# Latent norms, rotary keys and S5's angles and step table worked out under the first projection

## What is computed

```python
h = rmsnorm(x, norm_mix[layer])
z = h @ e_w_in[li]                      # 1024 -> 512 (u) + 384 (xq) + 256 (xkv) + 32 (kr)
u, xq, xkv, kr = z[..., :o1], z[..., o1:o2], z[..., o2:o3], z[..., o3:]
y_s5, hr, hi = s5_mixer(u, ...)         # diagonal state space: h[t] = a * h[t-1] + x[t], a complex
...
def mla_project(xq, xkv, kr, pos, q_norm, w_uq, kv_norm):
    q = jnp.einsum('ntr,rhd->nthd', rmsnorm(xq, q_norm), w_uq)
    ...
    ckv = rmsnorm(xkv, kv_norm)
    k_rope = rope(kr, pos, MLA_THETA)
...
def s5_mixer(...):
    dt = jnp.exp(log_dt)[:, None]
    mag = jnp.exp(lr * dt)
    ar = mag * jnp.cos(li * dt)
    ai = mag * jnp.sin(li * dt)
```

## Time and profile before

| | us |
|---|---|
| median of 3 runs | 3492.07 (3490.07 to 3496.64) |
| profiled execution | 3496.9 |
| its span, from the first to the last instruction | 3494.7 |
| PE busy | 3119.3 (89%) |
| DVE busy | 1784.7 (51%) |
| ACT busy | 693.3 (20%) |
| POOL busy | 878.2 (25%) |

### The profile page before, as it was taken

The page is one execution under the profiler, slowest core; times in us unless marked ns, Lnnn a source line. Parts: engine busy times, 40 slices in busy tenths (PEclk is TensorE's granted clock), DMA queues, the critical chain, the costliest instruction groups (busy, mean ns, idle before and its releaser), DMA issues. The chain is left out here.

```text
span 3494.7 us, 58782 instructions
## 1 busy us (share of the span) xinstructions
PE 3119.3 (89%) x21927; PEld 2794.6 (80%) x21927; DVE 1784.7 (51%) x2928; ACT 693.3 (20%) x1443; POOL 878.2 (25%) x496
## 2 busy tenths in 40 slices
PE   7736788888888888899999999999879999999996
PEld 7623465666676666899999999999549999999996
DVE  4288264554645555365244343566774643525254
ACT  2010132333323332121000000110551210000001
POOL 3100000000001110444343434442004444344332
PEclk9867899999989998999999999999989999999998
DMA  2000100010056664211111111120211111111112
GB/s 99 12 14 15 42 12 13 0 37 0 0 161 195 195 194 122 97 57 47 44 48 44 49 40 55 39 67 25 80 55 51 55 39 51 44 53 41 49 41 70
DMA packets 129070, 205.44 MB, mean 59 GB/s; under 512 B 14817, under 2 KB 95713, under 8 KB 128258
## 3 DMA queue, kind: packets, MB, share of 16 engines
q1 hardware_dynamic: 127810, 199.81, 18.9%
q10 hardware_dynamic: 1152, 4.23, 0.3%
HBM read 189.61 MB, written 6.25 MB: 56 GB/s over the span
## 5 line engine op out<-in xcount | busy, mean ns | idle before, releaser
L136 PE MATMUL ps_trunk_out<-sb_h_hi,sb_slab_hi 128*128 128x344 f32 x2400 | 768.0, 320 | 0.0
L137 PE MATMUL ps_trunk_out<-sb_h_hi,sb_slab_lo 128*128 128x344 f32 x2400 | 764.8, 319 | 0.0
L138 PE MATMUL ps_trunk_out<-sb_h_lo,sb_slab_hi 128*128 128x344 f32 x2400 | 764.4, 319 | 0.0
L120 POOL TENSOR_TENSOR sb_slab_hi<-sb_slab_raw,sb_ones 128x1024 fp32r<-128x1024 f32 (+3 forms) x214 | 345.7, 1616 | 1361.2 <-PE ps_trunk_out L138 1051.6
L122 POOL TENSOR_TENSOR sb_slab_lo<-sb_slab_raw,sb_slab_hi 128x1024 fp32r<-128x1024 f32 (+3 forms) x214 | 485.7, 2270 | 16.8
L137 PEld LDWEIGHTS ps_trunk_out<-sb_h_hi,sb_slab_lo 128*128 128x128 f32 x2400 | 450.4, 188 | 0.6
L136 PEld LDWEIGHTS ps_trunk_out<-sb_h_hi,sb_slab_hi 128*128 128x128 f32 x2400 | 450.3, 188 | 0.6
L138 PEld LDWEIGHTS ps_trunk_out<-sb_h_lo,sb_slab_hi 128*128 128x128 f32 x2400 | 450.4, 188 | 0.0
L1314 POOL TENSOR_TENSOR sb_dec_kr<-sb_dec_ck,sb_ones 128x256 f32<-128x256 f32 x64 | 46.7, 729 | 1199.4 <-DMA sb_dec_ck<-cache 1103.1
L136 PE MATMUL ps_trunk_out<-sb_ffn_a_hi,sb_slab_hi 128*128 128x344 f32 x1056 | 336.9, 319 | 4.9 <-DVEq L1586 4.9
L138 PE MATMUL ps_trunk_out<-sb_ffn_a_lo,sb_slab_hi 128*128 128x344 f32 x1056 | 337.9, 320 | 0.0
(11 more groups left out here) (386 smaller groups left out, 5163.2 us busy)
## 6 DMA issues: line engine op xcount, KB each, us to landing
sb_dec_ck<-cache SPq DMA_DIRECT2D x512, 144.0 KB, 2.4
sb_slab_raw<-f_w_gu SPq DMA_DIRECT2D x88, 512.0 KB, 3.5
sb_slab_raw<-f_w_down SPq DMA_DIRECT2D x32, 384.0 KB, 3.1
sb_slab_raw<-f_w_down SPq DMA_DIRECT2D x32, 320.0 KB, 2.9
sb_slab_raw<-e_w_out SPq DMA_DIRECT2D x24, 256.0 KB, 2.6
sb_slab_raw<-o_w_in SPq DMA_DIRECT2D x12, 512.0 KB, 3.4
sb_slab_raw<-e_w_in SPq DMA_DIRECT2D x10, 512.0 KB, 3.3
sb_x_first<-x SPq DMA_DIRECT2D x8, 516.0 KB, 8.4
```

Source lines behind the costliest of these rows:

```text
L120: nc.gpsimd.tensor_tensor(hi, raw, one, ALU.mult).then_inc(self.hi_done[s], 1)
L136: nc.tensor.matmul(out[:, t, 0:TT], a, x_hi(k)[:, cols], start=k == 0, stop=False)
L137: nc.tensor.matmul(out[:, t, 0:TT], b, x_hi(k)[:, cols], start=False, stop=False)
L138: last = nc.tensor.matmul(out[:, t, 0:TT], a, x_lo(k)[:, cols], start=False, stop=k == kc - 1)
```

## The change

The three pieces of work leave their places and stand in the block of the first projection. The ten tiles come in the sequence 4 to 9, then 0 to 3 (`tile(q) = (q + 4) % 10`), so both latents and the key come first. The loops over tiles are written out.

- SP loads S5's parameters first of all, issues the key's part of the rotary table (32 partitions, `kr_rot`) when the step table is done, and stores latent and key in this block.
- ACT and DVE work out the angles before the first norm.
- DVE doubles the table between evacuations: six doublings behind the first, the seventh behind the second, and the eighth in two halves behind the third and fourth. The result goes where x lay. Then come the sums of squares of the latents (PE's sums over the partitions stand inside tiles 6 and 7), the scalings behind evacuations 5 and 6, and the key's rotation behind evacuation 7. The swap of the halves is now a shuffle on DVE and not a product on PE.
- S5's block keeps the rest. The key rotation's block is gone, and the attention's block loads the full rotary table between mask and weights.

```diff
+        pc, psn, nps = (small("s5_" + n, [P, NPOW, NTILE5]) for n in ("pc", "ps", "nps"))
...
+            swap_lanes = [q ^ 16 for q in range(32)]
+            thirds = [slice(t * TT, (t + 1) * TT) for t in range(3)]
+            evacuated = lambda eng, q: eng.wait_ge(slabs.free[q % 2], n0 + q // 2 + 2)
...
             with nc.Block() as block:
                 @block.sync
                 def _(sp):
+                    sp.dma_start(par[:, :, :], A["s5_par"]).then_inc(par_in, 16)
                     for k in range(KD):
                         sp.dma_start(x[:, k, :], A["x"][k]).then_inc(norm_x_in[k], 16)
                         if k < 2:
-                            slabs.load(sp, k, n0, KD, A["e_w_in"][k])
-                    with sp.Fori(0, 4) as i:
-                        for s in range(2):
-                            slabs.load(sp, s, i + (n0 + 1), KD,
-                                       A["e_w_in"][bass.ds(i * 2 + s + 2, 1)].rearrange("a p k m -> p (a k) m"))
+                            slabs.load(sp, k, n0, KD, A["e_w_in"][tile(k)])
+                    for q in range(2, 10):
+                        slabs.load(sp, q % 2, q // 2 + n0, KD, A["e_w_in"][tile(q)])
+                        if q == 7:
+                            sp.wait_ge(tab_done, 1)
+                            sp.dma_start(kr_rot[:, :, :], A["rot_mla"][0:ROPE]).then_inc(kr_in, 16)
+                    sp.wait_ge(lat_done, 2)
+                    store(sp, O["ckv"].rearrange("c p t -> p c t"), z[:, 7:9, :])
+                    sp.wait_ge(kr_done, 1)
+                    store(sp, O["krope"], z[0:ROPE, 9, :])
...
-                    with pe.Fori(0, 4) as i:
-                        for s in range(2):
-                            slabs.products(pe, s, i + (n0 + 1), KD, hi, lo)
+                    def lat_sums(i, a, *ts):
+                        pe.wait_ge(lat_added, (2, 3)[i])
+                        for t in ts:
+                            if t == 2:
+                                pe.wait_ge(lat_root, 3 * i + 1)
+                            nc.tensor.matmul(tot(t), ones[:, :], a[:, thirds[t]], start=True, stop=True).then_inc(lat_sum, 1)
+                    hooks = {0: paced(pe, 0),
+                             1: {1: lambda: (norm_sums(pe, 0, acc, tot, 0), norm_sums(pe, 0, acc, tot, 1)),
+                                 4: lambda: norm_sums(pe, 0, acc, tot, 2)},
+                             6: {1: lambda: lat_sums(0, q_acc, 0, 1), 4: lambda: lat_sums(0, q_acc, 2)},
+                             7: {3: lambda: lat_sums(1, kv_acc, 0, 1), 6: lambda: lat_sums(1, kv_acc, 2)}}
+                    for q in range(10):
+                        if q == 6:
+                            pe.wait_ge(norm_root, 3)
+                        if q == 7:
+                            pe.wait_ge(lat_root, 3)
+                        slabs.products(pe, q % 2, n0 + q // 2, KD, hi, lo, hooks[q] if q in hooks else ())
                 @block.scalar
...
+                    ch = Chain(act, act_chain, chain_at["act"])
+                    act.wait_ge(par_in, 16)
+                    nc.scalar.activation(dtv, par[:, 2, :], ACT.Exp).then_inc(dt_done, 1)
+                    act.wait_ge(th_done, 1)
...
+                    nc.scalar.activation(pc[:, :, :], pc[:, :, :], ACT.Sin, scale=-1.0,
+                                         bias=halfpi[:, 0:1]).then_inc(trig_done, 1)
+                    chain_at["act"] = ch.n
                     for k in range(KD):
                         act.wait_ge(norm_x_in[k], 16)
                         norm_act(act, 0, k, x[:, k, :], gain(k), acc[:, :], sq[:, :])
                     norm_roots(act, 0, tot, D)
+                    for q, dst in enumerate((q_acc, q_r, kv_r, kv_acc, sq)):
+                        evacuated(act, q)
+                        if q == 4:
+                            act.wait_ge(tab_done, 1)
+                        nc.scalar.activation(dst[:, :], z[:, 4 + q, :], ACT.Square).then_inc(lat_sq, 1)
+                    for i, (r, width) in enumerate(((q_r, QL), (kv_r, KVL))):
+                        for t in range(3):
+                            act.wait_ge(lat_sum, 3 * i + t + 1)
...
                     for k in range(KD):
                         norm_dve(dve, 0, k, x[:, k, :], gain(k), acc[:, :], sq[:, :])
                     norm_inverse(dve, ch, 0)
+                    def evacuate(q):
+                        dve.wait_ge(slabs.mm_done[q % 2], n0 + q // 2 + 2)
+                        V.tensor_tensor(v3(z[:, tile(q), :]), slabs.out[:, q % 2, :, 0:TT], v3(rstd),
+                                        ALU.mult).then_inc(slabs.free[q % 2], 1)
+                    def double(j, n0, n1):
+                        n = n1 - n0
+                        pcb, psb = (v[:, 2 + j, :].unsqueeze(2).broadcast_to((P, NTILE5, n)) for v in (pc, psn))
+                        w = [t[:, 0:NTILE5 * n].rearrange("p (a b) -> p a b", b=n) for t in tmp]
+                        c0, s0 = tab[:, 0, :, n0:n1], tab[:, 1, :, n0:n1]
+                        step = 1 << j
+                        V.tensor_tensor(w[0], c0, pcb, ALU.mult)
+                        V.tensor_tensor(w[1], s0, psb, ALU.mult)
+                        V.tensor_tensor(w[2], c0, psb, ALU.mult)
+                        tt(w[3], s0, pcb, ALU.mult)
+                        V.tensor_tensor(tab[:, 0, :, step + n0:step + n1], w[0], w[1], ALU.subtract)
+                        tt(tab[:, 1, :, step + n0:step + n1], w[2], w[3], ALU.add)
+                    def added(i, a, s, n):
+                        dve.wait_ge(lat_sq, n)
+                        if i:
+                            dve.wait_ge(lat_added, i)
+                        V.tensor_tensor(a[:, :], a[:, :], s[:, :], ALU.add).then_inc(lat_added, 1)
+                    def scale(i, r, c0, cols, g0):
+                        for t in range(3):
+                            dve.wait_ge(lat_root, 3 * i + t + 1)
+                            ch.mark(V.reciprocal(r[:, thirds[t]], r[:, thirds[t]]))
+                        ch.settle()
+                        for c in range(cols):
+                            m = V.scalar_tensor_tensor(out=z[:, c0 + c, :], in0=z[:, c0 + c, :], scalar=gq[:, g0 + c:g0 + c + 1],
+                                                       in1=r[:, :], op0=ALU.mult, op1=ALU.mult)
+                        m.then_inc(lat_done, 1)
+                    evacuate(0)
+                    dve.wait_ge(trig_done, 1)
+                    V.memset(tab[:, 0, :, 0:1], 1.0)
+                    ch.link(V.memset(tab[:, 1, :, 0:1], 0.0))
+                    for j in range(6):
+                        double(j, 0, 1 << j)
+                    evacuate(1)
+                    double(6, 0, 64)
+                    evacuate(2)
+                    double(7, 0, 64)
+                    evacuate(3)
+                    double(7, 64, 128)
+                    dve.sem_inc(tab_done, 1)
+                    added(0, q_acc, q_r, 2)
+                    added(1, q_acc, kv_r, 3)
+                    evacuate(4)
+                    added(2, kv_acc, sq, 5)
+                    evacuate(5)
+                    scale(0, q_r, 4, 3, 0)
+                    evacuate(6)
+                    scale(1, kv_r, 7, 2, 3)
+                    evacuate(7)
+                    dve.wait_ge(kr_in, 16)
+                    kr = z[0:ROPE, 9, :]
+                    ch.link(V.stream_shuffle(kr_s[:, :], kr, swap_lanes))
+                    tt(kr_t[:, :], kr, kr_rot[:, 0, :], ALU.mult)
+                    tt(kr_s[:, :], kr_s[:, :], kr_rot[:, 1, :], ALU.mult)
+                    V.tensor_tensor(kr, kr_t[:, :], kr_s[:, :], ALU.add).then_inc(kr_done, 1)
+                    evacuate(8)
+                    evacuate(9)
                     chain_at["dve"] = ch.n
...
-        norm_phase("n_q", lambda k: z[:, 4 + k, :], 3, QL, lambda k: gq[:, k:k + 1], plain=lambda k: z[:, 4 + k, :])
-        norm_phase("n_kv", lambda k: z[:, 7 + k, :], 2, KVL, lambda k: gq[:, 3 + k:4 + k], plain=lambda k: z[:, 7 + k, :])
...
                 @block.sync
                 def _(sp):
-                    for dst, src in ((par[:, :, :], "s5_par"), (bw[:, :, :, :], "s5_b"), (cw[:, :, :, :], "s5_c"),
+                    for dst, src in ((bw[:, :, :, :], "s5_b"), (cw[:, :, :, :], "s5_c"),
                                      (dskip[:, :], "s5_d"), (h0[:, :, :, :], "s5_h0")):
...
                     dve.wait_ge(ca_done, 1)
-                    for j in range(8):
-                        n = 1 << j
-                        pcb, psb = (v[:, 2 + j, :].unsqueeze(2).broadcast_to((P, NTILE5, n)) for v in (pc, psn))
-                        w = [t[:, 0:NTILE5 * n].rearrange("p (a b) -> p a b", b=n) for t in tm]
-                        tc0, ts0 = tab[:, 0, :, 0:n], tab[:, 1, :, 0:n]
-                        V.tensor_tensor(w[0], tc0, pcb, ALU.mult)
-                        V.tensor_tensor(w[1], ts0, psb, ALU.mult)
```

(15 more changed lines are left out.)

199 lines of the change are left out of this document (68 added, 131 removed).

## The result

| | kernel before | changed kernel |
|---|---|---|
| median, us | 3491.07 (3489.93 to 3496.64) | 3429.17 (3425.60 to 3433.76) |
| profiled execution, us (its span) | 3496.64 (3494.7) | 3433.76 (3431.9) |
| ratio after/before | | 0.9823, 95% interval 0.9811 to 0.9835 |

A forecast was written before the change was run, and what follows sets the result against it. TensorE (PE) bounds the kernel (89% busy) and the first projection; terms -37.5 - 0.4 - 25.0 - 9.7 + 1.3 + 4.1 + 7.7 + 1.6 + 0.4 = -57.5 us; 3492.07 - 57.5 = 3434.6 us, range 3422 to 3446.

The forecast's parts named there:

- (a): Behind the first projection: the two latent norms leave the path, -37.5 us.
- (b): S5's angles behind its loads: taking them out gains nothing, one DMA issue fewer ahead of the loads gives -0.4 us.
- (c): Ahead of S5's first step: the table's 48 DVE operations go, but DVE then waits for PE's first states, -25.0 us.
- (d): Between gate and attention: the key rotation's block goes, but the rotary table now queues ahead of the weights, -9.7 us.
- (e): Ahead of the first norm: exponentials, angles and sines now stand before ACT's first product, +1.3 us, bounds 0 and 3.0.
- the replay: Ahead of the first norm: DVE's and POOL's turns replayed with ACT 3.0 us late, third low part 1.3 us later.
- (f): Latent sums: three products with ones inside each of two projection tiles, +4.1 us for both.
- (g): First projection: doublings blocked by POOL's splits make evacuations late; PE waits +7.7, slow clock +1.6, later wait +0.4 us.
- R1: First projection: doublings not blocked, or POOL gives way, so the late evacuations cost nothing; 3425 us, chance 15%.
- R2: Terms at their bad ends, with load and weights sharing the queue slowly; gain 52, 3440 us, chance 12%.
- R3: First projection: PE's clock falls at tile 3's wait and doesn't return; slower than before, 3500 us, chance 2%.
- R4: End of projection: the second norm's end or the rotation hangs behind the last tile; gain about 40, 3452 us, chance 3%.

## Why the prediction was right, and where not

- **Norms (a), -37.5.** 43.43 - 5.66 = 37.8 with the load's front of (b) in it, and 37.1 with the norms put back. Right.
- **S5 behind the loads (b), -0.4.** Last evacuation to landing is 5.66 us in the changed kernel (5.5 to 6.0 over the nine other profiles without a norm there and without this load) and 6.3 with the angles' parameters loaded there again. The angles themselves cost nothing there (73.6 us with and without). Right.
- **Table (c), -25.0.** 73.68 - 48.49 = 25.2, and 25.1 by putting it back. The step that made it 25 and not 30.9, that PE's first states were beneath the table and would be late next, is the 5.56-us wait at 207.58. One slip in a bound: by its own rates, 64 x 0.066 = 4.2 us from 226.25, the states would have ended 1.4 us earlier, not 1.5.
- **Key rotation (d), -9.7.** 18.32 - 8.56 = 9.8, and 17.8 - 8.56 = 9.3 by putting it back. What it is made of was a little off: the rotary table costs some 2.1 us in the queue (8.35 to 8.99 from gate to attention in nine profiles with it there, 6.3 and 6.6 in two without), not 2.6 to 3.0.
- **Ahead of the first norm (e), +1.3.** 0.7 to 0.8. The bound 0 to 3 held it, but the mechanism was wrong: the replay let ACT come 3.0 late and kept POOL's turns nearly where they were. ACT was 2.6 late, yet POOL's first split had moved by 0.71 (9.92 instead of 9.21) and DVE's third low part by 0.76 with it, and a profile whose slab landed 1.3 us later still had everything 1.3 later. The term that the replay lacked is the later landing of the first slab.
- **Sums (f), +4.1.** 3.55 by the kernel without them, six products of 0.59 us each (16 of the same shape lasted 9.41), where the prediction had 0.66 from a row of two.
- **Late evacuation (g), +7.7 + 1.6 + 0.4.** The mechanism is shown by the run without splits. The sizes were off in both directions: the wait is 6.5 to 6.7, since the two meetings with POOL cost some 3.8 us each and not 4.3, as DVE's row starts a little behind POOL's; the clock costs 3.0, not 1.6, because the low level lasted 5.4 us behind this wait, and 3.5 us behind the shorter pause of the earlier trace rows, from which the price was taken; and tile 6 waits 0, because the split behind tile 3 (81.14) misses the doubling that I had let it meet. Tile 3 ended where the working had it (80.2, and 0.8 for the later start), since the shorter wait and the longer slow part make up for each other, but DVE's doubling had gained from the shorter meetings alone and was in its last row. Evacuation 3 starts at 81.94, not near 88, and evacuation 4 at 98.86. With the clock kept up the meeting comes back, and so does a wait of 0.67 us at tile 6. The three parts together were 9.7 in the forecast and 9.5 to 9.7 in the trace. That they agree so well is luck: an error of -1.1, one of +1.4 and one of -0.4.
- **The sum.** -57.5 was forecast for what ends with attention's start, and -58.8 came; the single terms were each within 1.4 us. The forecast of 3434.6 was 5.4 above the measured 3429.17: 1.3 from there, 1.0 from the median of before that was taken, and some 3 that lie behind attention's start, where the prediction had nothing and where the kernels scatter by more.
- **The rivals.** R1 (no blocking) is refuted: DVE's rows beside a split took 1.85 to 2.82 us, and tile 3 waited. Its price was right: without the splits the kernel gains 9.4 us more, where it had 9.7. R2, R3 and R4 didn't come: attention starts 8.56 behind the gate; the clock is back before tile 3 ends; the last evacuation waits 8.80 us for TensorE.
- **A rule of the Trainium skill (SBUF — State Buffer, Who interferes with whom)** said that the second of two contending instructions waits for the whole of the first. By it (g) stood at 9.7; the rows at 49.24 and 51.15 (1.85 and 2.42 us instead of 0.21) agree, with broadcast operands of 64 elements too.
- **The other (ScalarE: Activation LUTs, What ACT_TABLE_LOAD costs)**, a drain of some 1380 ns beside the load, would have made the sum 1.4 us worse. No run here shows that drain; its only sight is the earlier trace rows, where the sine starts 1.29 us behind the load's start. In the changed kernel the sine waits for DVE, so its rows can't tell, but (e) came out smaller than forecast, not larger.

## What to carry to other kernels

Work that is moved into an idle engine's gaps is worth what it cost on the path less what it had covered there; both can be read from the stretch before the change. Its price is set by the one row with a deadline that ends up behind it: here small DVE rows ahead of an evacuation, each held up by a GpSimd split beside it. Order such rows by deadline, keep the evacuations first, and leave the last piece to a wait that exists anyway; and when one wait goes, look what the engines meet in its place, since with DVE 82% busy under the projection a gain of 9.4 us at tile 5 was 5.5 at the end.

## What the runs showed of the hardware that was not expected

- DVE rows of 64 elements a partition, 0.21 us alone, take 1.85 and 2.42 us beside a split: the price of a meeting is what is left of the other engine's row, whatever the size of the one held up.
- After a wait of 6.7 us TensorE's granted clock stayed at its low level for 5.4 us of full work, 3.0 us of time. Products that keep it busy through the wait keep the clock at 1.00.
- One profile had its first slab of weights land 1.3 us later than the same instructions had it elsewhere, and carried these 1.3 us to evacuation 0. A preamble that waits for loads is best compared over several profiles.
- Without a changed instruction, attention took 1119 to 1132 us, over kernels and executions, while the feed-forward parts agreed to some tenths. Differences of under 5 us between kernels are better read from the stretch that was edited than from the whole time: 34.8 and 41.9 us are the same edit.
